# Opening of a hybrid attention trunk: x loaded with D on the partitions, its norm over partitions on TensorE, and fillers on TensorE while it waits

## What is computed

```python
c_act = silu(c)
shift, scale, gate = split(c_act @ w_ada + b_ada, 3)
h = rmsnorm(x, g_norm) * (1 + scale) + shift
q_sb, k_sb, v_sb, q_fx, k_fx, v_fx, g_path, f_logit = split(h @ w_in)
# 8 heads of stick-breaking attention, 8 heads of forgetting attention (head size 64)
y = concat(rmsnorm(o_sb, g_grp[:512]), rmsnorm(o_fx, g_grp[512:])) * silu(g_path)
x = x + (1 + gate) * (y @ w_out)
return rmsnorm(x, g_final)
```

## Time and profile before

| | |
|---|---|
| three executions | 792.29, 793.72, 795.7 us; median 793.72 |
| profiled execution | 790.59 us, span 788.8 |
| busy | PE 716.6 (91%), DVE 494.2 (63%), ACT 409.4 (52%), POOL 396.7 (50%) |
| PE busy by fortieths of the span, first eight | 0, 4, 9, 8, 7, 7, 9, 8 tenths |
| DMA | 91.57 MB, mean 116 GB/s |

### The profile page before, as it was taken

How to read it: one execution, slowest core, us unless ns; L and a number is a source line. 1 busy time by engine, 2 the same in 40 slices (tenths; PEclk the granted TensorE clock), 3 DMA queues, 4 the chain that set the end, 5 groups by cost and what they waited for, 6 DMA issues and landing times.

```text
span 788.8 us, 10998 instructions
## 1 busy us (share of the span) xinstructions
PE 716.6 (91%) x3936; PEld 600.0 (76%) x3936; DVE 494.2 (63%) x996; ACT 409.4 (52%) x848; POOL 396.7 (50%) x322
## 2 busy tenths in 40 slices
PE   0498779889999998999999899999998998999995
PEld 0376567778888887888888788888887887888884
DVE  3865956775565477656554866565567655645566
ACT  4523535675466564646675546457554557423222
POOL 4445406526878454467865535766566464221100
PEclk9999989999999999999999999999999999999999
DMA  8832410022334311023443001244331229792223
GB/s 348 323 108 80 134 27 28 27 82 95 107 108 144 110 55 39 1 95 107 147 148 106 27 27 53 78 154 144 133 114 51 64 91 346 220 325 99 81 89 125
DMA packets 34518, 91.57 MB, mean 116 GB/s; under 512 B 4248, under 2 KB 5912, under 8 KB 33952
## 3 DMA queue, kind: packets, MB, share of 16 engines
q1 hardware_dynamic: 27072, 70.56, 26.0%
q0 software_dynamic: 5376, 14.68, 5.9%
q10 hardware_dynamic: 2016, 5.63, 1.8%
HBM read 67.23 MB, written 23.63 MB: 115 GB/s over the span
## 4 chain that ended last, share of the span: by engine, by line
PE 59%; DVE 14%; ACT 9%; POOL 6%; issue 6%; DMA 5%; ACTq 0%; DVEq 0%; SPq 0%; POOLq 0%
PE psum L1446 10%; PE psum L1352 9%; PE psum L1357 9%; PE psum L1353 9%; PE psum L1434 7%; PE psum L1410 6%; DVE pt_lo L1014 3%; PE psum L1381 3%; DVE work L1094 3%; PE psum L1380 3%; DVE stacks L1062 3%; DMA w_raw<-in_w_blocks 2%; PE psum L1419 2%; DVE pt_lo L1154 2%; DMA w_f_raw<-in_w_f 2%
## 5 line engine op out<-in xcount | busy, mean ns | idle before, releaser
L1352 PE MATMUL psum<-h_hi,w_hi 128*128 128x512 f32 x496 | 208.2, 420 | 9.9 <-DVE stacks L1062 6.3
L1357 PE MATMUL psum<-h_hi,w_lo 128*128 128x512 f32 x496 | 196.4, 396 | 0.0
L1353 PE MATMUL psum<-h_lo,w_hi 128*128 128x512 f32 x496 | 195.3, 394 | 0.0
L653 POOL TENSOR_TENSOR work<-work 128x127 f32<-128x127 f32 (+3 forms) x64 | 79.4, 1242 | 169.0 <-DVE work L1094 169.0
L855 ACT ACTIVATE pt_hi<-psum 128x512 fp32r<-128x512 f32 (+1 forms) x192 | 87.6, 490 | 116.7 <-PE psum L1410 113.2
L1154 DVE TENSOR_TENSOR pt_lo<-psum,pt_hi 128x512 fp32r<-128x512 f32 (+1 forms) x192 | 100.6, 551 | 60.9 <-ACT pt_hi L855 59.4
L1094 DVE TENSOR_TENSOR_SCAN work<-work 128x128 f32<-128x128 f32 (+3 forms) x64 | 103.2, 1614 | 33.5 <-ACT work L823 33.4
L1352 PEld LDWEIGHTS psum<-h_hi,w_hi 128*128 128x128 f32 x496 | 94.9, 191 | 28.6 <-issue 9.2
L1357 PEld LDWEIGHTS psum<-h_hi,w_lo 128*128 128x128 f32 x496 | 94.2, 190 | 21.8
L1353 PEld LDWEIGHTS psum<-h_lo,w_hi 128*128 128x128 f32 x496 | 94.9, 191 | 16.1
L659 POOL TENSOR_SCALAR work<-work,small 128x128 f32<-128x128 f32 (+3 forms) x64 | 47.8, 747 | 91.7 <-DVE small L1117 91.5
(11 more groups left out here) (154 smaller groups left out, 1279.6 us busy)
## 6 DMA issues: line engine op xcount, KB each, us to landing
w_raw<-in_w_blocks SPq DMA_DIRECT2D x29, 512.0 KB, 4.2
work<-in_w_ada_t SPq DMA_DIRECT2D x18, 512.0 KB, 4.8
w_split_scratch<-work SPq DMA_DIRECT2D x16, 512.0 KB, 3.0
work<-in_x SPq DMA_DIRECT2D x12, 512.0 KB, 6.6
y_split_scratch<-work SPq DMA_DIRECT2D x10, 512.0 KB, 3.6
work<-forget_scratch SPq DMA_DIRECT2D x8, 512.0 KB, 5.0
work<-in_w_out SPq DMA_DIRECT2D x16, 256.0 KB, 3.1
stacks<-y_split_scratch POOLq DMA_DIRECT2D x4, 1024.0 KB, 6.8
```

Of the source, the lines that this page charges most:

```text
L653: nc.gpsimd.tensor_tensor(U[g % 2][:, 0:n - 1], U[g % 2][:, 0:n - 1], R[g % 2][:, 1:n], ALU.mult).then_inc(s_prob, 1)
L1352: nc.tensor.matmul(bank, hi, h_hi[:, c_, cols], start=(c_ == 0), stop=False)
L1353: last = nc.tensor.matmul(bank, hi, h_lo[:, c_, cols], start=False, stop=(kind == "f" and c_ == DC - 1))
L1357: last = nc.tensor.matmul(bank, lo, h_hi[:, c_, cols], start=False, stop=(c_ == DC - 1))
```

## The change

x comes a second time from the host, transposed (`x_t`, by half, D chunk, partition, position), in runs of 512 positions. Its squares are made by D chunk on ACT and summed over the partitions by PE: the square is the stationary operand, a column of ones the moving one. DVE turns the inverse roots into diagonal matrices (root times identity); PE multiplies a square of ones with them, which puts the roots of 512 positions on all partitions (`spread_roots`); ACT copies that out (`roots_down`). h is then made without transposes: DVE scales x (`scale_x`), ACT adds the shift and rounds (`h_piece`), DVE makes `h_lo`. f becomes the fourth unit of each half inside the pieces. ACT splits the first weights' high parts in place of DVE. The gate's columns and its store move into steps 1 to 9 of the loop's first pair; their weights are loaded there, into x's later space. Identity and mask are cast first, and PE multiplies the two with each other (`keep_busy`, results unused) 16 times at the start, 3 times after each but the last chunk of the first half's sums, 12 and 10 times around the first spread.

```diff
-    units = [(p, kind, h) for h in range(NHALF) for p, kind in blocks[:N_FIRST - 1]]
-    units += [(-1, "f", h) for h in range(NHALF)]
+    units = [(p, kind, h) for h in range(NHALF) for p, kind in blocks[:N_FIRST]]
...
+            def load_x(th, j):
+                sp.dma_start(x_room(th, 2 * j),
+                             x_t[th, 2 * j:2 * j + 2].rearrange("c p n -> p c n")).then_inc(s_x[4 * th + j], 16)
+            for j in range(4):
+                load_x(0, j)
+            for n in range(2):
                 load_ada(n)
+            sp.dma_start(w_early[:, 0], w_block(0, "k")).then_inc(s_wearly[0], 16)
+            sp.dma_start(w_early[:, 1], w_block(0, "v")).then_inc(s_wearly[1], 16)
+            for n in range(2, 4):
+                load_ada(n)
+            for j in range(4):
+                load_x(1, j)
+            for n in range(4, 2 * DC):
+                load_ada(n)
+            load_w(N_FIRST)
+            for n in range(2 * DC, 2 * DC + LATE_SLOTS):
+                load_ada(n)
...
+                if p == 0 and GATE_FROM <= i < GATE_FROM + DC - LATE_SLOTS:
+                    load_ada(2 * DC + LATE_SLOTS + i - GATE_FROM)
+                if p == 0 and i == GATE_FROM + DC:
+                    store_gate()
...
+            def x_squares(th):
+                for d in range(DC):
+                    n = th * DC + d
+                    if d % 2 == 0:
+                        act.wait_ge(s_x[n // 2], 16)
+                    if n >= 2:
+                        act.wait_ge(s_xsum, n - 1)
+                    nc.scalar.activation(x_sq[:, n % 2, :], x_tile(th, d), ACT.Square).then_inc(s_xsq, 1)
+            def roots_down(h):
+                act.wait_ge(s_rdown, h + 1)
+                nc.scalar.activation(roots[:, h, :], psum[:, ROOT_BANK[h], :], ACT.Copy).then_inc(s_rall, 1)
             def h_piece(n):
+                act.wait_ge(s_xscaled, n + 1)
+                nc.scalar.activation(h_hi[:, d, th * HALF:(th + 1) * HALF], spare[:, n % 2, :], ACT.Identity,
                                      bias=ada[:, d:d + 1]).then_inc(s_hhi, 1)
...
+            split_first_w(0)
+            x_squares(0)
+            split_first_w(1)
             x_roots(0)
+            split_first_w(2)
+            roots_down(0)
+            split_first_w(3)
             for n in range(2 * DC):
+                if first_pieces[n] == (0, 2):
+                    x_squares(1)
+                if first_pieces[n] == (1, 0):
                     x_roots(1)
+                    roots_down(1)
                 h_piece(n)
...
+            def scale_x(n):
+                dve.wait_ge(s_rall, th + 1)
+                dve.wait_ge(s_acol, d + 1)
+                if n >= 2:
+                    dve.wait_ge(s_hlo, n - 1)
+                nc.vector.scalar_tensor_tensor(out=spare[:, n % 2, :], in0=x_tile(th, d), scalar=a_cols[:, d:d + 1],
+                                               in1=roots[:, th, :], op0=ALU.mult, op1=ALU.mult).then_inc(s_xscaled, 1)
+            def h_lo_piece(n):
                 dve.wait_ge(s_hhi, n + 1)
+                nc.vector.scalar_tensor_tensor(out=h_lo[:, d, cols], in0=spare[:, n % 2, :], scalar=ada[:, d:d + 1],
+                                               in1=h_hi[:, d, cols].bitcast(fp32), op0=ALU.add,
+                                               op1=ALU.subtract).then_inc(s_hlo, 1)
...
+            x_roots(0)
+            columns(0)
+            scale_x(0)
+            columns(1)
+            h_lo_piece(0)
+            scale_x(1)
+            columns(2)
+            h_lo_piece(1)
+            for n in range(2, 2 * DC):
+                if first_pieces[n] == (1, 0):
                     x_roots(1)
+                scale_x(n)
+                if first_pieces[n][0] == 0 and first_pieces[n][1] + 1 < DC:
+                    columns(first_pieces[n][1] + 1)
+                h_lo_piece(n)
+            for u in (0, 1, 3):
+                proj_out(u)
             scores_out(0)
             scores_out(1)
+            for u in (4, 5, 7):
+                proj_out(u)
...
+                if p == 0 and GATE_FROM <= i < GATE_FROM + DC:
+                    ada_column(2 * DC + i - GATE_FROM)
...
+            def sum_x_squares(th):
+                for d in range(DC):
+                    pe.wait_ge(s_xsq, th * DC + d + 1)
+                    for t in range(4):
+                        last = nc.tensor.matmul(psum[:, SUM_BANK[th], t:t + 1],
+                                                x_sq[:, d % 2, t * P:(t + 1) * P], ones,
+                                                start=(d == 0 and t == 0), stop=(d == DC - 1 and t == 3))
+                    last.then_inc(s_xsum, 1)
+                    if th == 0 and d < DC - 1:
+                        keep_busy(3)
+            def spread_roots(th):
+                pe.wait_ge(s_diag, th + 1)
+                nc.tensor.matmul(psum[:, ROOT_BANK[th], :], ones_square[:], root_diag[:, th, :], start=True,
+                                 stop=True).then_inc(s_rdown, 1)
+            def keep_busy(n):
+                for _ in range(n):
+                    nc.tensor.matmul(psum[:, ROOT_BANK[1], 0:2 * P], ident_bf[:],
+                                     mask_bf[:].rearrange("p a n -> p (a n)"), start=True, stop=True)
+            pe.wait_ge(s_maskb, 2)
+            keep_busy(16)
+            pe.wait_ge(s_ones, 1)
+            sum_x_squares(0)
+            keep_busy(12)
+            spread_roots(0)
+            keep_busy(10)
+            for n in range(2 * DC):
+                if first_pieces[n] == (0, 2):
+                    sum_x_squares(1)
+                if first_pieces[n] == (1, 0):
+                    spread_roots(1)
+                first_piece(n)
```

More of the change, by code:

```diff
@@ L255, in hybrid_trunk_kernel @@
         s_x = [sem(f"s_x{i}") for i in range(TB)]
-        s_wa = [sem(f"s_wa{i}") for i in range(7)]
+        s_xsq = sem("s_xsq")
+        s_xsum = sem("s_xsum")
+        s_diag = sem("s_diag")
+        s_rdown = sem("s_rdown")
+        s_rall = sem("s_rall")
+        s_xscaled = sem("s_xscaled")
+        s_wa = [sem(f"s_wa{i}") for i in range(9)]
         s_c = sem("s_c")
@@ L266, in hybrid_trunk_kernel @@
         s_rn = sem("s_rn")
-        s_xn = [sem(f"s_xn{i}") for i in range(2)]
-        s_xt = sem("s_xt")
         s_hhi = sem("s_hhi")
-        s_hf = [sem(f"s_hf{i}") for i in range(2)]
         s_hlo = sem("s_hlo")
@@ L908, in _ @@
             scores_out(1)
-            for u in range(4, 2 * N_FIRST):
+            for u in range(N_FIRST, 2 * N_FIRST):
                 proj_out(u)
@@ L1026, in norm_columns @@
                                                op0=ALU.add, op1=ALU.mult).then_inc(s_acol, 1)
-            for b in range(N_FIRST):
-                split_first_w(b)
             dve.wait_ge(s_const, 16)
@@ L1418, in sum_squares @@
                 for t in range(TB):
-                    last = nc.tensor.matmul(bank[:, t:t + 1], squares[:, t * P:(t + 1) * P], ones[:], start=True, stop=True)
+                    last = nc.tensor.matmul(bank[:, t:t + 1], squares[:, t * P:(t + 1) * P], ones, start=True, stop=True)
                 last.then_inc(s_t, 1)
@@ L1540 @@
     batch, seq, d = x.shape
+    x_t = np.ascontiguousarray(x[0].reshape(2, seq // 2, d // 128, 128).transpose(0, 2, 3, 1))
     w_in = np.asarray(w_in)[0]
```

255 lines of the change are left out of this document (94 added, 161 removed).

## The result

The changed kernel took 802.53 us in the median of four runs (801.70 to 803.45), the one before 794.28: ratio 1.0106, interval 1.0082 to 1.0131. It is 1.1% slower. The forecast was 789.1 with a range of 781 to 800, so the time lies outside it, and nearest to the first rival (798.9). The profiled executions took 801.7 (span 799.7) and 790.59 (788.8), 10.9 us apart in the span; all that follows is laid against that.

The account below looks back on a forecast made before the run. Before the loop PE was taken to follow DVE, so an earlier loop start (96.5 for 103.45) counts in full: -7.0, load past the gate store -1.6, gate columns +4.0, sum -4.6 us, forecast 789.1, range 781 to 800.

Parts of the forecast that it names:

- the first rival: Opening: sums run at half rate, 2.4 us a chunk, loop starts at 106.3; +5.2, 798.9 us, slower; chance 0.20.
- a chunk costs PE 1.22 at the full rate: First sums: products 0.88 plus three fillers 0.34 us a chunk, so PE sets the pace and sums end at 20.4.
- the 16 fillers are dense: Opening, from 6.6 us: argument against half-rate sums; the fillers last 3.4 us at half rate and fit before the sums.
- Squares, loads, first weights: Opening: ACT copies weights (1.15 us), squares from 9.5 at 0.6 each; x landed by some 12; sums from 10.1.
- Roots and spread: After the first sums: mean, root, diagonals 0.7, spread 0.9, copy 0.7, DVE's columns and scaling; first piece at 28.0.
- Pieces 0 and 1: First-half pieces on DVE: scale 0.65, two columns with the norm 2.75, h_lo 0.65 each; both end at 35.4.
- Second sums: PE's sums for the second half, queued behind piece 1: 8 x 0.88 = 7.0 us, to 42.5.
- From there to the first scaling of the second half: Before the second half's scaling: piece 2's h_lo done at 42.9, roots 2.4, spread and copy 1.7 us, reaching 47.0.
- Pairs: From 47.0, a pair of pieces costs DVE 6.3 us, handover to ACT included; four pairs end at 72.2.
- Load of the weights past the gate's store: Loop: block 5's load no longer stands behind the gate store; gain 1.6 us, bounds 0 and 2.7.
- Gate columns in the loop: Pair 0, steps 1 to 8: eight columns before DVE's pt_lo; 4.0 us lost, bounds 0 and 9.8 (18.5 beside POOL).
- the one named last: Loop: DVE's gate columns contend with POOL's SBUF reads, per the skill; rival "loop pays", +1.2, 794.9 us, chance 0.20.

Follow-up runs that it names:

- early splits: Changed kernel with ACT's copies of the second to fourth first weight blocks ahead of the first half's root; median 799.85 us, 1.0061 of the kernel before.
- the reordered kernel: Changed kernel with fp32r sums, gate columns moved off steps 5 and 6, DVE's opening reordered, second sums in two blocks; median 783.12 us, 0.9857 of the kernel before.

## Why the prediction was wrong

**The step that failed** is "a chunk costs PE 1.22 at the full rate", taken for seven of the eight chunks, and with it the end of the first sums at 20.4. The size at the full rate was right (1.14 measured, where PE had that rate). The rate was not. In the profiled execution the chunk is 2.16 us, the sums end at 26.75 (+6.3), the first piece starts at 35.80 instead of 28.0. It is what the first rival said (2.4 a chunk, the sums over at 28.2, "the spread takes 0.8 more"), with a chance of 0.20 (by its own 2.4 a chunk the sums end at 28.6, not 28.2); the argument against it, "the 16 fillers are dense", weighed the fillers as proof of a rise that nothing in the trace showed. I had read in the earlier trace rows that up to 31.86 PE went at half rate, and still put the full rate at 11 us. Nor would the step have held with the rise where I put it: in the five profiles where the full rate came near 10 us, the clock fell again under the sums, and they ended at 22.9 to 24.4 and not at 20.4. Why the rise comes near 10 us in some executions and after 33 in others stays open.

The other terms, in the order of the sum:
- Squares, loads, first weights: right. PE's first chunk starts at 9.93, forecast 10.1.
- Roots and spread: from the end of the sums to the first piece 9.05 us, forecast 7.6. One of the four diagonals took 2.34 us instead of 0.28, beside POOL's split (2.34 us long), and the spread took the half rate (2.08 us). The sum priced POOL beside the columns and not beside the roots.
- Pieces 0 and 1: 7.6 us, forecast 7.4.
- Second sums: 11.8 us, forecast 7.0 (+4.8). Even the first rival, as I wrote it, left these at the full rate, which is one reason why its 798.9 fell short. The clock falls under them (0.50 from 46 to 58).
- From there to the first scaling of the second half: 6.1 us, forecast 4.5; piece 2 now runs at the half rate.
- Pairs 6.14, forecast 6.3; from that scaling to the last remainder 35.7 us, forecast 36.4. Then 12.5 to the loop, forecast 13.1.

6.3 + 1.5 + 0.2 + 4.8 + 1.6 - 0.7 - 0.6 = 13.1, against 12.9 between 96.5 and 109.44.
- Load of the weights past the gate's store: -1.8 at step 3, forecast -1.6. Right. The slow start of the loop gave another 0.7.
- Gate columns in the loop: +2.2 at step 7 and +2.0 of half rate behind it, forecast +4.0. The size came out, in part by luck: 2.2 are tied to the columns in every profile, while a half-rate stretch of 1.5 came at step 12 without any column. The reason was the one named last: not DVE's gaps but contention with POOL. It lengthened POOL's product beside a column in other steps too (2.22 us for 128x639, 1.31 before), but PE waited only for the chain before step 7. The Trainium skill's section Who interferes with whom (SBUF — State Buffer), cited there, agrees in kind: the pairs that met are those it names. What the runs add is where the price is paid, in POOL's chain (0.9 and 1.0 us) that PE waits for.
- Stretches at a lower clock at steps 40 and 104, 3.2 us together: not in the forecast. Twelve of the fourteen runs' profiles lose 2.6 to 3.5 us behind step 14 in this way, half of them at steps 40 and 104, the others at steps 72 and 117; the ones without sum fillers and with early splits lose some 0.2 or less. Why they fall where they do isn't settled.

The marks given for the working were loop start before 93 or after 100, and it was 109.44: the forecast named itself wrong, and named the line (products of sums 0.22 apart: they are 0.20).

## What to carry to other kernels

A cost on TensorE taken from one stretch of a trace holds at that stretch's clock; before it is moved into an opening or under tiny products, count it at both rates, and forecast by the one that the rows beside the new place show. Work of tiny products was made cheap here by fewer instructions (fp32r with two columns instead of fp32 with one: 0.9967 of the kernel before instead of 1.0067), not by fillers around it (1.0041 to 1.0064). And an addition to an engine that looks idle is placed by what the neighbour engine does in those steps: the same eight products opened a wait of 2.2 us at step 7 or none.

## What the runs showed of the hardware

- The record of the granted clock says 1.00 from the start, while PE works at half rate (fillers of 256 columns 0.21 apart, later 0.107) until it first reaches the full one. With the same opening that came near 10 us in some profiles and after 33 in others (the changed kernel's last ten fillers still take 2.12 us from 33.36, its first piece at 35.80 is at the full rate). In the loop's start the two forms are 4.6 to 4.9 us apart (104.53 and 104.82 against 109.44); with eight fillers a chunk the executions fell into two groups 12 us apart.
- Under products of one column with three fillers a chunk the clock fell (0.50 from 14 to 24); with eight, in the one profile, it didn't. The fall also came under the second sums and in the middle of piece 1 of the reordered kernel.
- One small DVE instruction can wait out a whole POOL instruction. Of the changed kernel's eight diagonals, minimum, median and maximum in ns:

```profile
L1002 DVE TENSOR_SCALAR pt_hi_early<-ident,small x8: 274/281/2340, 28.5 to 57.5; 128x128 f32<-128x128 f32 x8
```

Beside two of POOL's splits of 2.35 us, two products of 128x4 took 2.04 and 2.26 us instead of 0.16 in the fp32r run, and with early splits one that began halfway through a split took 1.22. In each case it ended with the split, so the price was what was left of POOL's instruction, not the size of DVE's.
